# A two-block transformer kernel on one core: the first product fed from raw transposed rows, and the setup transposes packed into two

## What is computed

```python
def rms_norm(x, g):
    xf = x.astype(jnp.float32)
    y = xf * lax.rsqrt(jnp.mean(xf * xf, axis=-1, keepdims=True) + EPS)
    return (y * g.astype(jnp.float32)).astype(x.dtype)

def swiglu_ffn(h, w13, w2):
    gate, up = jnp.split(h @ w13, 2, axis=-1)
    return (jax.nn.silu(gate) * up) @ w2
...
x = x + 0.5 * swiglu_ffn(rms_norm(x, ffn1_norm[l]), ffn1_w13[l], ffn1_w2[l])
```

## Time and profile before

| | us |
|---|---|
| median of 3 runs | 1243.76 |
| the three runs | 1242.35, 1243.76, 1244.33 |
| the profiled execution's own time | 1245.61 |
| its span, first to last instruction | 1243.9 |

### The profile page before, as it was taken

The page is one execution under the profiler, slowest core; times in us unless marked ns, Lnnn a source line. Parts: engine busy times, 40 slices in busy tenths (PEclk is TensorE's granted clock), DMA queues, the critical chain, the costliest instruction groups (busy, mean ns, idle before and its releaser), DMA issues.

```text
span 1243.9 us, 16425 instructions
## 1 busy us (share of the span) xinstructions
PE 1231.9 (99%) x6535; PEld 1058.4 (85%) x6535; DVE 784.8 (63%) x935; ACT 622.3 (50%) x798; POOL 76.9 (6%) x127
## 2 busy tenths in 40 slices
PE   8999999999999999999999999999999999999998
PEld 7888888998888888899999888888888888888887
DVE  4666546897755655677677666554678637566545
ACT  5444426665544444655623544543566845444433
POOL 1000002002000000400001000000024000000000
PEclk9999999999999999999999999999999999999999
DMA  8988755551688774545202398875366417887740
GB/s 278 315 247 250 242 196 155 177 172 58 195 260 238 242 257 151 188 137 173 82 1 63 123 290 250 257 230 192 143 213 207 138 56 248 253 255 234 237 135 34
DMA packets 172108, 235.35 MB, mean 189 GB/s; under 512 B 13785, under 2 KB 127325, under 8 KB 172028
## 3 DMA queue, kind: packets, MB, share of 16 engines
q1 hardware_dynamic: 172032, 234.30, 58.9%
HBM read 221.67 MB, written 12.58 MB: 188 GB/s over the span
## 4 chain that ended last, share of the span: by engine, by line
PE 92%; DVE 3%; ACT 2%; POOL 1%; DMA 0%; issue 0%; SPq 0%; ACTq 0%; DVEq 0%; POOLq 0%
PE bank L1580 28%; PE bank L1582 27%; PE bank L1581 27%; PE bank L1977 2%; PE bank L1988 1%; PE bank L1614 1%; DVE y L1178 1%; DVE wlo L1060 1%; PE bank L1950 1%; PE bank L1943 1%; PE bank L1904 1%; PE bank L1996 1%; DMA raw<-in_ffn_w_dram 0%; ACT whi L426 0%; PE bank L2082 0%
## 5 line engine op out<-in xcount | busy, mean ns | idle before, releaser
L1060 DVE TENSOR_TENSOR wlo<-raw,whi 128x2048 fp32r<-128x2048 f32 (+1 forms) x190 | 416.4, 2195 | 249.5 <-ACT whi L426 249.4
L426 ACT ACTIVATE whi<-raw 128x2048 fp32r<-128x2048 f32 x190 | 363.1, 1915 | 227.1 <-PE bank L1582 219.3
L1580 PE MATMUL bank<-whi,xThi 128*128 128x512 f32 x1024 | 402.9, 393 | 2.5 <-DVE xTlo L1083 1.0
L1582 PE MATMUL bank<-whi,xTlo 128*128 128x512 f32 x1024 | 399.9, 390 | 0.0
L1581 PE MATMUL bank<-wlo,xThi 128*128 128x512 f32 x1024 | 399.4, 390 | 0.0
L1580 PEld LDWEIGHTS bank<-whi,xThi 128*128 128x128 f32 x1024 | 192.8, 188 | 43.2 <-DVE xTlo L1522 1.5
L1582 PEld LDWEIGHTS bank<-whi,xTlo 128*128 128x128 f32 x1024 | 192.5, 188 | 40.5
L1581 PEld LDWEIGHTS bank<-wlo,xThi 128*128 128x128 f32 x1024 | 192.9, 188 | 38.9
L1580 PE MATMUL bank<-whi,hThi 128*128 128x512 f32 x352 | 137.4, 390 | 0.0
L1582 PE MATMUL bank<-whi,hTlo 128*128 128x512 f32 x352 | 137.1, 389 | 0.0
L1581 PE MATMUL bank<-wlo,hThi 128*128 128x512 f32 x352 | 137.1, 389 | 0.0
(11 more groups left out here) (395 smaller groups left out, 1176.5 us busy)
## 6 DMA issues: line engine op xcount, KB each, us to landing
raw<-in_ffn_w_dram SPq DMA_DIRECT2D x176, 256.0 KB, 4.4
raw<-in_ffn_w_in_dram SPq DMA_DIRECT2D x176, 256.0 KB, 4.1
raw<-in_ffn_w_dram SPq DMA_DIRECT2D x22, 1024.0 KB, 5.4
raw<-in_ffn_w_out_dram SPq DMA_DIRECT2D x22, 1024.0 KB, 5.3
raw<-in_gdn_w_in_dram SPq DMA_DIRECT2D x16, 1024.0 KB, 5.4
hidden<-hblk SPq DMA_DIRECT2D x44, 256.0 KB, 5.1
hraw<-hidden SPq DMA_DIRECT2D x176, 64.0 KB, 3.3
raw<-in_w_in_dram SPq DMA_DIRECT2D x10, 1024.0 KB, 5.1
```

What stands on the lines that cost most here:

```text
L426: act.activation(whi[w % SPLIT][:], raw[w % RAW][:], ACT.Copy).then_inc(w_hi, 1)
L1060: dve.tensor_tensor(wlo[w % SPLIT][:, c], raw[w % RAW][:, c], whi[w % SPLIT][:, c].bitcast(F32), ALU.subtract).then_inc(w_lo, 1)
L1580: pe.matmul(psum, lhs[0], rhs[0], start=start, stop=False, skip_group_check=True)
L1582: return pe.matmul(psum, lhs[1], rhs[0], start=False, stop=stop, skip_group_check=True)
```

## The change

The first product takes x as it is: both tiles are transposed raw, the norm's weights are brought to the partitions by one small transpose (gain_col) and multiplied in as a scale per partition when ACT and DVE copy the transposed rows out; the root of the norm, one number per row, is applied behind the product, in Silu's scale and in the multiplication by the up columns, for all 11 blocks of this layer. A copy covers 256 columns (both tiles of one k) and each k of the product is done for both tiles at once. The squares and the root move behind the pieces of slot 1. The broadcast load of the norm's weights goes (and with it later loads into gain0 start at n = 2 without a wait), a load of 8 rows comes; tile 1 of x is loaded ahead of the weights. Three slots instead of two are split in pieces. PE's warm-up has 14 products and the three between go. For the setup, conv_w with conv_b and gdn_conv_2 are loaded as 128 and 96 rows of 128 channels, and two transposes bring them over; tap and tap4 have their axes swapped, chan is a part of tap.

```diff
-    WARM = 11
+    WARM = 14
...
-        chan = sb("chan", [P, CT])
-        tap = sb("tap", [P, CT, TAPS])
-        tap4 = sb("tap4", [P, QKV, W4])
+        tap = sb("tap", [P, TAPS + 1, CT])
+        chan = tap[:, TAPS]
+        tap4 = sb("tap4", [P, W4, QKV])
...
-        FIRST, PIECES = 2, 4
+        FIRST, PIECES = 3, 4
...
-                sp.dma_start(row_chan[:], a["conv_b"][0].rearrange("(c p) -> c p", p=P)).then_inc(done, 16)
-                sp.dma_start(row_tap[:], a["conv_w"][0]).then_inc(done, 16)
-                sp.dma_start(row_tap4[:], a["gdn_conv_2"][0]).then_inc(done, 16)
+                sp.dma_start(row_tap[TAPS * CT:, :], a["conv_b"][0].rearrange("(c p) -> c p", p=P)).then_inc(done, 16)
+                sp.dma_start(row_tap[0:TAPS * CT, :], a["conv_w"][0].rearrange("k (c p) -> (k c) p", p=P)).then_inc(done, 16)
+                sp.dma_start(row_tap4[:], a["gdn_conv_2"][0].rearrange("k (c p) -> (k c) p", p=P)).then_inc(done, 16)
...
-                if w < NT:
-                    sp.dma_start(X[:, w, :], a["x"][0, w * P:(w + 1) * P, :]).then_inc(sem(f"x_in{w}"), 16)
+                if w == 0:
+                    for t in range(NT):
+                        sp.dma_start(X[:, t, :], a["x"][0, t * P:(t + 1) * P, :]).then_inc(sem(f"x_in{t}"), 16)
+                        if t == 0:
+                            sp.dma_start(row_gain[:], NORM[0].rearrange("(k p) -> k p", p=P)).then_inc(sem("first_gain"), 16)
...
+                        if f == 0:
+                            act.wait_ge(sem("norm_rstd"), nth(0, t))
+                        act.activation(hnat[:, j % 2, t, :], bank[2 * (j % 2) + t][:, 0:256], ACT.Silu,
+                                       scale=1.0 if f else rstd[:, t:t + 1]).then_inc(sem("ffn_silu"), 1)
...
+            def first_hi(k):
+                act.wait_ge(sem("first_T"), k + 2 - k % 2)
+                if k == 0:
+                    act.wait_ge(sem("first_col"), 1)
+                act.activation(xThi[:, k, :], bank[4 + k // 2][:, (k % 2) * SEQ:(k % 2 + 1) * SEQ], ACT.Copy,
+                               scale=gain_col[:, k:k + 1]).then_inc(sem("first_hi"), 1)
+
+            first_hi(0)
+            first_hi(1)
+            for n in range(KD // 2 - 1):
+                piece_hi(0, n)
+                first_hi(2 * n + 2)
+                first_hi(2 * n + 3)
+            for n in range(KD // 2 - 1, FIRST * PIECES):
+                piece_hi(n // PIECES, n % PIECES)
+                if n == 2 * PIECES - 1:
+                    norm_sum(0, 0, sem("x_in0"), 16)
+                    norm_sum(0, 1, sem("x_in1"), 16)
...
+                            dve.scalar_tensor_tensor(out=h, in0=up, scalar=rstd[:, t:t + 1], in1=h,
+                                                     op0=ALU.mult, op1=ALU.mult).then_inc(sem("ffn_h"), 1)
...
+            def first_lo(k):
+                dve.wait_ge(sem("first_hi"), k + 2 - k % 2)
+                dve.scalar_tensor_tensor(out=xTlo[:, k, :], in0=bank[4 + k // 2][:, (k % 2) * SEQ:(k % 2 + 1) * SEQ],
+                                         scalar=gain_col[:, k:k + 1], in1=xThi[:, k, :].bitcast(F32),
+                                         op0=ALU.mult, op1=ALU.subtract).then_inc(sem("first_lo"), 1)
+
+            dve.wait_ge(sem("first_gain_T"), 1)
+            dve.tensor_copy(gain_col[:], bank[3][:, 0:KD]).then_inc(sem("first_col"), 1)
+            dve.wait_ge(sem("first_col"), 1)
+            first_lo(0)
+            first_lo(1)
+            for n in range(KD // 2 - 1):
+                piece_lo(0, n)
+                first_lo(2 * n + 2)
+                first_lo(2 * n + 3)
+            for n in range(KD // 2 - 1, FIRST * PIECES):
+                piece_lo(n // PIECES, n % PIECES)
...
-                pe.transpose(bank[7][:, 0:CT], row_chan[:], ident[0:CT, 0:CT])
-                for c in range(CT):
-                    pe.transpose(bank[7][:, 16 + c * TAPS:16 + (c + 1) * TAPS], row_tap[:, c * P:(c + 1) * P],
-                                 ident[0:TAPS, 0:TAPS])
-                for c in range(QKV):
-                    ins = pe.transpose(bank[7][:, 160 + c * W4:160 + (c + 1) * W4], row_tap4[:, c * P:(c + 1) * P],
-                                       ident[0:W4, 0:W4])
+                pe.transpose(bank[7][:, 0:P], row_tap[:], ident[:])
+                ins = pe.transpose(bank[7][:, P:P + W4 * QKV], row_tap4[:], ident[0:W4 * QKV, 0:W4 * QKV])
...
+            def first_turn():
+                pe.wait_ge(sem("first_gain"), 16)
+                pe.transpose(bank[3][:, 0:KD], row_gain[:], ident[0:KD, 0:KD]).then_inc(sem("first_gain_T"), 1)
+                for t in range(NT):
+                    pe.wait_ge(sem(f"x_in{t}"), 16)
+                    for k in range(KD):
+                        at = (k % 2) * SEQ + t * P
+                        ins = pe.transpose(bank[4 + k // 2][:, at:at + P], X[:, t, k * P:(k + 1) * P], ident[:])
+                        if t:
+                            ins.then_inc(sem("first_T"), 1)
...
+                for h in range(2):
+                    for k in range(4):
+                        pe.wait_ge(sem("first_lo"), 4 * h + k + 1)
+                        pe.wait_ge(w_lo, split_done(h, k))
+                        for t in range(NT):
...
+                            if h == 1 and k == 3 and t == 0:
+                                ins.then_inc(sem("ffn_mm0"), 1)
+                    ins.then_inc(w_used, 1)
```

More of the change, by code:

```diff
@@ L193, in build_program @@
              ("pp", [P, NT, D], F32)],
[L194 removed]
+            [("row_tap", [P, P], F32), ("row_tap4", [W4 * QKV, P], F32), ("row_gain", [KD, P], F32)])
         hdram = [nc.dram_tensor(f"hidden{i}", [P, 4, P], F32, kind="Internal").ap() for i in range(2)]
@@ L432, in norm_sum @@
                 act.wait_ge(ready, value - (not whole))
-                i = turn(f"n{max(n, 4) if n == FINAL else n}")
-                if i and n not in (FINAL, FINAL + 1):
-                    act.wait_ge(sem("turn_T"), 4 * (i - 1) + 2 * t + 2)
+                if n > 1 and n not in (FINAL, FINAL + 1):
+                    act.wait_ge(sem("turn_T"), 4 * (turn(f"n{n}") - 1) + 2 * t + 2)
                 if n == FINAL + 1:
@@ L538, in diagonals @@
                             ins = act.activation(diag[:, CT * k + c, :], ident[:], ACT.Copy,
-                                                 scale=tap[:, c, TAPS - PE_TAPS + k:TAPS - PE_TAPS + k + 1])
+                                                 scale=tap[:, TAPS - PE_TAPS + k, c:c + 1])
                     return ins
@@ L870, in piece_hi @@
                 act.activation(whi[w][:, c], raw[w][:, c], ACT.Copy).then_inc(w_hi, 1)
-            def first_hi(t, b):
-                act.wait_ge(sem("turn_T"), 2 * t + b + 1)
-                act.activation(xThi[:, 4 * b:4 * b + 4, t * P:(t + 1) * P], bank[4 + b][:].rearrange("p (k c) -> p k c", k=4),
-                               ACT.Copy).then_inc(sem("turn_hi"), 1)
-            norm_sum(0, 0, sem("x_in0"), 16)
-            piece_hi(0, 0)
-            piece_hi(0, 1)
-            first_hi(0, 0)
-            piece_hi(0, 2)
-            first_hi(0, 1)
-            piece_hi(0, 3)
-            norm_sum(0, 1, sem("x_in1"), 16)
-            for k in range(PIECES):
-                piece_hi(1, k)
-            first_hi(1, 0)
-            first_hi(1, 1)
+            def first_hi(k):
[15 more added lines that the diff above has]
+                    norm_sum(0, 1, sem("x_in1"), 16)
             ffn(0)
@@ L2180, in first_block @@
                                          h == 0 and k == 0, h == 1 and k == 3)
-                        if t:
-                            ins.then_inc(w_used, 1)
-                        elif h:
-                            ins.then_inc(sem("ffn_mm0"), 1)
+                            if h == 1 and k == 3 and t == 0:
+                                ins.then_inc(sem("ffn_mm0"), 1)
+                    ins.then_inc(w_used, 1)
             pe.wait_ge(*once("consts"))
             for i in range(WARM):
-                pe.matmul(bank[7][:, 0:P], ones[:], ident[:], start=True, stop=True)
-            first_turn(0, 0)
-            first_turn(0, 1)
-            for i in range(3):
-                pe.matmul(bank[7][:, 0:P], ones[:], ident[:], start=True, stop=True)
+                pe.matmul(bank[2][:, 0:P], ones[:], ident[:], start=True, stop=True)
+            first_turn()
             wide("down0", hT, ffn(0), next_turn("n1"))
```

85 lines of the change are left out of this document (22 added, 63 removed).

## The result

The changed kernel takes 1249.79 us (median of 4 runs, 1249.50 to 1250.05) against 1243.76 for the kernel before (median of 3 runs, 1242.35 to 1244.33; a fourth, at 2515.68 and far outside all others, is left out). The ratio is 1.0051, 95% interval 1.0038 to 1.0064: slower by 6 us, where I had forecast 3.8 us less.

What follows compares the result with a forecast made beforehand. PE, busy 99%, was taken to bound the kernel. From the median, 1243.76 - 1.2 (start) - 1.7 (setup) - 0.85 (half the clock dip) = 1240.0 us, chance 0.45; range 1238.0 to 1242.7.

Steps and rivals of the forecast that it cites:

- The gain should reach the end whole: Whole kernel: time won at start and setup stays won to the end, as PE is busy 99%.
- All that I cost at nothing: Beyond the first block: slot waits and splits, more descriptors, root timing and extra multiplications were all given 0 us.
- rival 4: First block: low clock throughout as PE repeatedly meets idle, 48 products take 20.6 us, total 1249.7; chance 0.03.
- Part 1: Start of first block: first product later, at 11.75, then dense, ending at 22.8 against 23.97; 1.2 us gained, bounds 0.6 and 2.3.
- the 9.65 of my sum: Start of first block: ACT begins copying the transposed rows at about 9.65 us, after transposes starting at 8.15.
- Part 2: Blocks 1 and 2: slot 2 ready by 22.5 at latest, needed 22.8; slot 4 at 33.37, needed 33.7; both covered.
- Part 3: Setup from 45.83 to 47.71: 29 transposes become two, taking 0.3 us instead of 1.97; 1.7 us gained, bounds 1.5 and 1.8.
- Part 4: Behind setup: the 3.40 us stretch at 1.2 GHz goes, 1.7 us gained, counted half (0.85) for the median.
- Rival 1: Start: clock drops to 1.2 GHz for a stretch, 1.5 us lost, first block gains nothing, 1241.5; chance 0.27.
- The stretch at 499: From 499.48 to 502.89: products, eight transposes and 1.3 us idle kept clock 1.00, so no dip forecast at the start.
- rival 2: Start and setup: earlier clock rise makes the start worth 2.3 us, full dip in median run, 1238.1; chance 0.13.
- rivals 1 and 3: Rival 1, and a new wait for slot 2 or 4 giving 1 to 1.5 us back, 1241.3, chance 0.12.

Runs made afterwards that it cites:

- a_level_back: The changed kernel with the spacer level put back from 32 to 40 columns, restoring the old tile addresses: 1242.68 us, ratio 0.9991 to the kernel before.
- b_level_moved: The kernel before with only the spacer level cut from 40 to 32 columns, so everything behind starts 32 bytes lower: 1251.04 us, ratio 1.0058.
- a_first_only: The changed kernel's new start with the 29 setup transposes of before, all tiles at the old addresses: 1243.05 us, ratio 0.9995.

## Why the prediction was wrong

**The step that failed** is "The gain should reach the end whole, since PE is busy 99% and everything behind is paced by it". It took the products behind the change to cost what they did before, a term put at nothing without a reason. "All that I cost at nothing" covered waits, splits and descriptors; the smaller tap and spacer were in no sum at all, since I took the names and sizes of tiles for bookkeeping. In their place the runs show that moved tiles cost 7.1 us (a_level_back) to 7.7 us (b_level_moved), more than everything that the change wins: the lead of 3.82 us at 54 us is 3.9 us behind at the end. With it the sum of the trace closes. At 0.0066 for each of the 1056 hidden products the loss is 7.0 us, and the third mixer and the embedding products add some 0.9: 1245.61 - 0.34 - 1.84 - 1.7 + 7.9 = 1249.6, and the profiled execution took 1249.50. The side was lost here, and the chance of 0.03 for slower stood on another mechanism: rival 4, low clock for the whole first block, is in no trace.

**Part 1** was mis-sized: 0.34 us in place of 1.2. The transposes did start at 8.2 behind the warm-up, as worked out. Two things came after. ACT's table load, 1.28 us, had stood ahead of everything; now it stood behind ACT's first waits and ended at 9.95, some 0.45 us after the data was there and 0.3 after the 9.65 of my sum. And the copies with a scale per partition are dearer than their nearest rows. Timeline of the start of the kernel after:

```profile
8.31 1.97 PE L2162 MATMUL bank<-ident,X 128*128 128x128 f32 x16
8.67 1.28 ACT L884 ACT_TABLE_LOAD   x1 [8.67 <-DVE gain_col L1531]
9.96 0.84 ACT L884 ACTIVATE xThi<-bank,gain_col 128x256 fp32r<-128x256 f32 x2
10.69 0.63 ACT L878 ACTIVATE whi<-raw 128x512 fp32r<-128x512 f32 x1
10.91 0.88 DVE L1526 SCALAR_TENSOR_TENSOR xTlo<-bank,gain_col,xThi 128x256 fp32r<-128x256 f32 x2 [2.32 <-ACT xThi L884]
11.70 0.68 DVE L1522 TENSOR_TENSOR wlo<-raw,whi 128x512 fp32r<-128x512 f32 x1
12.53 0.47 PE L1580 MATMUL bank<-whi,xThi 128*128 128x512 f32 x1 [2.25 <-DVE wlo L1522]
```

Two copies take 0.84 us and not 0.64, two low parts 0.88 and not 0.74. Per k DVE needs 1.39 us (pieces at 11.70, 13.09, 14.47, 15.86) against PE's 1.36, so the block is dense to 0.2 us. A last 0.15 us lies between the first piece's wlo, done at 12.38, and the product. The price was inside the bound that I gave for it; the table load was thought of, but for the squares, as one "that Copy alone did not need". It stands before the first Copy.

**Part 2** held: no wait for slot 2 or slot 4; slot 4 was there at 27.40, not 29.13. **Part 3** held, 1.84 for 1.7, just over its bound of 1.8. **Part 4** held: none of the seven traces with the two transposes has a dip behind setup, and six of the thirteen with the 29 have one. So the 29 bring it in some executions only, and counting half a dip for the median was right in kind. The sum named only one of the two dips in the trace that it started from; the other, from 537.02, is in the trace of the change too (536.84).

**Rival 1** happened in one execution traced: a_first_only's low stretch at 13.07 to 16.49. It is not in the trace of the change itself, where the clock stayed at 1.00 over the transposes and 2.25 us of idle. By the Trainium skill's rule on transposes (TensorE: Matmul & The Clock Gate, Part 4: PE-mode transpose) it would have fallen there; it did not. Whether in a_first_only the transposes or the idle time behind them brought it down, no run tells apart. The stretch at 499 that the prediction leaned on had 0.85 us of idle by its row (3.41 less 2.56 busy), not 1.3.

**The chances.** By its own terms, forecast nearly all, rival 2, half of rivals 1 and 3, the chance of faster adds up to about 0.75, not to the 0.68 that stands there. It would not have changed the side.

## What to carry to other kernels

Before a diff is costed instruction by instruction, list where every tile starts in SBUF before and after it; a tile of another size moves all that lie behind, and a spacer without a reader is a sign that it matters. Where matmuls of 512 columns set the time, let the starts of their two operands lie a multiple of 256 bytes apart; putting all of them at multiples of 256 does it. When a kernel's executions differ by equal steps, compare those at the same granted clock first, and look at what PE does in a stretch in which it must wait: filling it with work of no use is worth a try, to be measured.

## What was not expected of the hardware

- A 512-column fp32r product costs 5 to 7 ns of 227 more when its two operands start 32, 64, 96, 128 or 224 bytes (modulo 256) apart, and nothing when both are 32 bytes off together. Products of 256 columns lost nothing in any run, and gained some 3 ns with x moved alone.
- 1.8 us of products of no use ahead of the first real one took the ratio to the kernel before from 0.9991 to 0.9971 (medians 1242.7 and 1239.6, on two chips); with an earlier start they gave nothing (1240.6 with and without).
- Every low stretch of the clock behind setup or near 534 us began 1.4 to 3.4 us after the start of a run of products of at most 31 columns, though PE is shown as busy all that time, and it came in some executions only.
- The quickest versions are the change with the old addresses and the filling (ratio 0.9971), and that with the early start (0.9970 and, unfilled, 0.9974); the setup part alone gives 0.9982.
